# Setup of a decoder-trunk kernel: loads reordered over two queues, squares moved between the transposes, semaphores cleared by range

## The reference, cut to what matters

```python
mod = silu(c) @ w_mod[l] + b_mod[l]           # shift, scale, gate, 2 x 3 x 1024 columns, 9 vectors c
h = rms_norm(x, norm_mix[l]) * (1 + scale) + shift
x = x + gate * mixer(h)                       # layer 0: h @ ab_w_in first
```

## Time and profile before

| | us |
|---|---|
| runs (3) | 2413.52, 2416.56, 2420.88; median 2416.56 |
| the profiled execution | 2417.96 |
| its span, first to last instruction | 2416.3 |
| PE busy in the span | 2071.7 (86%) |
| DVE, ACT, POOL busy | 1360.7, 787.1, 272.1 |
| mean granted clock of PE | 0.913 |
| moved by DMA | 322.60 MB |

### The profile page before, as it was taken

The page is one execution under the profiler, slowest core; times in us unless marked ns, Lnnn a source line. Parts: engine busy times, 40 slices in busy tenths (PEclk is TensorE's granted clock), DMA queues, the critical chain, the costliest instruction groups (busy, mean ns, idle before and its releaser), DMA issues. The chain is left out here.

```text
span 2416.3 us, 48234 instructions
## 1 busy us (share of the span) xinstructions
PE 2071.7 (86%) x18117; PEld 1865.8 (77%) x18117; DVE 1360.7 (56%) x2556; ACT 787.1 (33%) x1407; POOL 272.1 (11%) x436
## 2 busy tenths in 40 slices
PE   4987797688999897997879996989987776999898
PEld 2873574386999896895569886988974475999898
DVE  3435431257888643446365657777743357888732
ACT  2211331114555301212246654544431214545300
POOL 0101333200000000000022212212223200000000
PEclk8996898798999998998789997999988898999999
DMA  8416789735333221224420004333449612333231
GB/s 345 131 45 254 246 294 365 283 111 159 97 98 106 96 87 40 62 83 181 174 91 1 2 1 145 112 105 113 118 140 339 237 62 70 105 100 93 90 96 62
DMA packets 237726, 322.60 MB, mean 134 GB/s; under 512 B 18235, under 2 KB 194440, under 8 KB 230063
## 3 DMA queue, kind: packets, MB, share of 16 engines
q1 hardware_dynamic: 215767, 240.34, 30.6%
q0 software_dynamic: 21728, 79.19, 9.5%
HBM read 311.56 MB, written 16.42 MB: 136 GB/s over the span
## 5 line engine op out<-in xcount | busy, mean ns | idle before, releaser
L2557 PE MATMUL ps<-CHi,W1H 128*128 128x256 f32 x768 | 221.7, 289 | 38.0 <-DVE CLo L2660 38.0
L2558 PE MATMUL ps<-CLo,W1H 128*128 128x256 f32 x768 | 219.7, 286 | 0.0
L2559 PE MATMUL ps<-CHi,W1L 128*128 128x256 f32 x768 | 219.5, 286 | 0.0
L897 PE MATMUL ps<-XHup,WLup 128*128 128x272 f32 x640 | 185.1, 289 | 0.0
L897 PE MATMUL ps<-XHup,WHup 128*128 128x272 f32 x640 | 183.8, 287 | 1.3 <-DVE G L1046 1.3
L897 PE MATMUL ps<-XLup,WHup 128*128 128x272 f32 x640 | 184.5, 288 | 0.0
L2557 PEld LDWEIGHTS ps<-CHi,W1H 128*128 128x128 f32 x768 | 150.0, 195 | 40.0 <-DVE CLo L2660 29.6
L443 PE MATMUL ps<-XHdn,WHdn 128*128 128x272 f32 x704 | 148.2, 292 | 14.7 <-DMA TOK<-in_cache_fox_v 6.5
L2078 DVE TENSOR_REDUCE NM<-ps 128x1 f32<-128x128 f32 (+1 forms) x224 | 89.6, 403 | 116.4 <-PE ps L1957 80.4
L2558 PEld LDWEIGHTS ps<-CLo,W1H 128*128 128x128 f32 x768 | 150.1, 195 | 0.0
L2559 PEld LDWEIGHTS ps<-CHi,W1L 128*128 128x128 f32 x768 | 149.9, 195 | 0.0
(11 more groups left out here) (562 smaller groups left out, 5339.6 us busy)
## 6 DMA issues: line engine op xcount, KB each, us to landing
H<-in_w_up SPq DMA_DIRECT2D x72, 512.0 KB, 4.9
Wearly<-in_w_mod SPq DMA_DIRECT2D x24, 1024.0 KB, 11.2
RAWdn<-in_w_down SPq DMA_DIRECT2D x14, 1408.0 KB, 6.3
RAWin<-in_nsa_w_in SPq DMA_DIRECT2D x20, 512.0 KB, 3.7
RINGf<-in_cache_fox_k SPq DMA_DIRECT2D x34, 256.0 KB, 5.6
Wmod<-in_w_mod SPq DMA_DIRECT2D x8, 1024.0 KB, 17.0
Wlate<-in_w_mod SPq DMA_DIRECT2D x8, 1024.0 KB, 8.3
G<-in_w_up SPq DMA_DIRECT2D x16, 512.0 KB, 5.4
```

Of the source, the lines that this page charges most:

```text
L897: last = self.nc.tensor.matmul(self.ps[:, bank + b, 0:HALF], wt[:, w, k, :], x[:, k, :], start=start and k == 0 and n == 0, stop=k == 3 an ...
L2557: nc.tensor.matmul(out, WH[:, sig, k, w], hi, start=(k == 0 and m == 0), stop=False, skip_group_check=True)
L2558: nc.tensor.matmul(out, WH[:, sig, k, w], lo, start=False, stop=False, skip_group_check=True)
L2559: last = nc.tensor.matmul(out, WL[:, sig, k, w], hi, start=False, stop=(k == KU - 1), skip_group_check=True)
```

## The change

Stages no longer clear their semaphores when they end. They are put on a list, and `flush`, called at the next stage's entry and at the end of the program, clears all of them in one block, with one `sem_clear` for each contiguous range of numbers.

In `setup`, SP issues the identity, the tokens, the ones, and the pieces of w_mod first; the first weight block comes as two halves (both in `self.first`), and the rest of the constants behind piece 1 of `Wearly`, under a semaphore of their own that the side job of the first projection waits for. The small vectors and the page table are issued by ACT. PE waits for identity, ones and tokens only, and for the vectors at k = 6. ACT makes every square into its own slice of H as soon as its group is there, and DVE adds them between the copies; scaling and page ids run in `root_dve`, while ACT computes the root. The bites before the first product are two instead of four, and `head_norm` takes 2 to 12 and loads 8 to 18.

```diff
@@ stage, clear
         nc = self.nc
+        self.flush()
         self.stages += 1
         number = self.stages
...
-            if made:
-                self.clear(made)
+        self.ended.append((semaphores, made))
+
+    def flush(self):
+
+        made = [s for _, m in self.ended for s in m]
+        if made:
+            self.clear(made)
+        while self.ended:
+            self.ended.pop()[0].close()
...
+                numbers = sorted(s.num for s in semaphores)
                 if drain:
-                    pool.dma_reset(range(min(s.num for s in semaphores), max(s.num for s in semaphores) + 1))
-                for s in semaphores:
-                    pool.sem_clear(s)
+                    pool.dma_reset(range(numbers[0], numbers[-1] + 1))
+                for a in numbers:
+                    if a - 1 not in numbers:
+                        pool.sem_clear(range(a, next(n + 1 for n in numbers if n >= a and n + 1 not in numbers)))
@@ setup, SP
-                    sp.dma_start(self.pages[:, :], i["page_table"].rearrange("(o b) n -> o (b n)", o=1)).then_inc(vec_in, 16)
-                    sp.dma_start(CN[:, :], i["const"][:, 0:CONST]).then_inc(c_in, 16)
...
+                    sp.dma_start(CN[:, 0:P], i["const"][:, 0:P]).then_inc(c_in, 16)
+                    sp.dma_start(XR[:, 0:4, :], i["x_prompt"][0].rearrange("(i p) d -> p i d", p=P)).then_inc(x_in, 16)
+                    sp.dma_start(XR[0:NS, 4, :], i["x_sample"].rearrange("b t d -> (b t) d")).then_inc(x_in, 16)
+                    sp.dma_start(CN[:, ones:ones + P], i["const"][:, ones:ones + P]).then_inc(c_in, 16)
                     for n in range(KD):
                         self.mod_load(sp, work, n)
-                    sp.dma_start(self.first_in[0], i["ab_w_in"][0:4 * P, 0:256].rearrange("(k p) n -> p k n", p=P)).then_inc(self.first_in[1], 16)
-                    for n in range(6):
+                    first_weights(sp, 0)
+                    for n in range(2):
+                        self.mod_load(sp, self.early, n)
+                    first_weights(sp, 1)
+                    sp.dma_start(CN[:, P:ones], i["const"][:, P:ones]).then_inc(self.const_in, 16)
+                    sp.dma_start(CN[:, ones + P:pmod - 1], i["const"][:, ones + P:pmod - 1]).then_inc(self.const_in, 16)
+                    for n in range(2, 6):
                         self.mod_load(sp, self.early, n)
@@ setup, ACT (12 DMAs are issued ahead of this: vectors, page table, pmod)
                     act.wait_ge(vec_in, 16 * n_vec)
                     nc.scalar.activation(R2[0:72, :], R2[0:72, :], ACT.Silu).then_inc(silu, 1)
                     for k in range(KD):
-                        act.wait_ge(xev, KD + 1)
-                        self.square(act, sums, k)
+                        act.wait_ge(xev, k + 2)
+                        nc.scalar.activation(self.H[:, k, :], X[:, k, :], ACT.Square).then_inc(sums["sq"], 1)
@@ setup, PE
-                    pe.wait_ge(c_in, 16)
-                    pe.wait_ge(vec_in, 16 * n_vec)
-                    nc.tensor.transpose(ps[:, 0, 0:P], R1[:, :], self.ident)
+                    pe.wait_ge(c_in, 32)
+                    pe.wait_ge(x_in, 32)
...
+                        if k == 6:
+                            pe.wait_ge(vec_in, 16 * n_vec)
+                            pe.wait_ge(silu, 1)
+                            nc.tensor.transpose(ps[:, 0, 0:P], R1[:, :], self.ident)
+                            nc.tensor.transpose(ps[:, 0, P:P + 82], R2[:, :], self.ident[0:82, 0:82]).then_inc(tr, 1)
@@ setup, DVE
+                    def square_sum(k):
+                        dve.wait_ge(sums["sq"], k + 1)
+                        link(nc.vector.tensor_tensor(self.H[:, self.SUM if k == KD - 1 else 0, :], self.H[:, 0, :], self.H[:, k, :], ALU.add))
...
                     for k in range(KD):
-                        dve.wait_ge(tr, k + 2)
+                        if k == 6:
+                            vectors_out()
+                        dve.wait_ge(tr, k + 2 + (k >= 6))
                         nc.vector.tensor_copy(X[:, k, 0:TP], ps[:, 2 + k % 6, :]).then_inc(xev, 1)
...
+                        if k >= 2:
+                            square_sum(k - 1)
+                    square_sum(KD - 1)
+                    dve.sem_inc(sums["added"], 1)
+                    self.root_dve(dve, link, root, small)
                     self.mod_add(dve, work, 0)
@@ fox_layer
-                self.linear("in", self.i["ab_w_in"], KD, 8, out=PT, norm=(0, 0), meal=(self.early, 0, 4, 4), first=self.first_in, root=self.root,
-                            more=lambda sp: [self.mod_load(sp, self.early, n) for n in range(6, 10)], beside=Forget(self, PT, NC, EP))
+                self.linear("in", self.i["ab_w_in"], KD, 8, out=PT, norm=(0, 0), meal=(self.early, 0, 2, 2), loaded=self.first_in, root=self.root,
+                            more=lambda sp: [self.mod_load(sp, self.early, n) for n in range(6, 8)], beside=Forget(self, PT, NC, EP))
...
-                               lambda sp: [self.mod_load(sp, self.early, n) for n in range(10, 19)], (self.early, 4, 13))
+                               lambda sp: [self.mod_load(sp, self.early, n) for n in range(8, 19)], (self.early, 2, 13))
```

More of the change, by code:

```diff
@@ L92, in __init__ @@
         self.stages = 0
+        self.ended = []
     @contextmanager
@@ L98, in stage @@
         nc = self.nc
+        self.flush()
         self.stages += 1
         number = self.stages
+        semaphores, made = ExitStack(), []
         with ExitStack() as held:
-            made = []
             def sb(name, shape, dt=F32):
@@ L107, in sem @@
             def sem(name):
-                made.append(held.enter_context(nc.semaphore(f"{name}_{number}")))
+                made.append(semaphores.enter_context(nc.semaphore(f"{name}_{number}")))
                 return made[-1]
             yield sb, sem
-            if made:
-                self.clear(made)
+        self.ended.append((semaphores, made))
[5 more added lines that the diff above has]
+            self.ended.pop()[0].close()
     def clear(self, semaphores, drain=True):
@@ L173, in setup, with first_weights @@
             work = self.mod_work("mod", sem, *meal_tile(sb("Wmod", [P, 512 + 8 * 2048])), [(0, 0)], [(4, 6)])
-            n_vec = 15
+            n_vec = 11
+            ones = 5 * P + 2 * NT + 4 * RUN
+            pmod = ones + P + PT_TILES * NCMP_P + 1 + NSEL + NS
+            def first_weights(sp, part):
+                sp.dma_start(self.first[:, part, :, :], i["ab_w_in"][part * 4 * P:(part + 1) * 4 * P, 0:256]
+                             .rearrange("(k p) n -> p k n", p=P)).then_inc(self.first_in[part], 16)
             with nc.Block() as block:
@@ L183, in _ @@
[L183 to L187, removed]
@@ L232, in _ @@
                         self.mod_bite(pe, work, n)
-                    pe.wait_ge(sums["added"], KD - 1)
+                    pe.wait_ge(sums["added"], 1)
                     self.root_pe(pe, root)
@@ L241, in _, with vectors_out @@
                     link = Chain(dve, dc)
+                    def square_sum(k):
+                        dve.wait_ge(sums["sq"], k + 1)
+                        link(nc.vector.tensor_tensor(self.H[:, self.SUM if k == KD - 1 else 0, :], self.H[:, 0, :], self.H[:, k, :], ALU.add))
+                    def vectors_out():
+                        dve.wait_ge(tr, 8)
+                        nc.vector.tensor_copy(VT[:, :], ps[:, 0, 0:P])
+                        nc.vector.memset(self.CV[:, :, :], 0.0)
+                        link(nc.vector.tensor_copy(CT[:, :], ps[:, 0, P:P + 82]))
+                        link(nc.vector.tensor_copy(self.CV[:, :, 0:9], CT[:, 0:72].rearrange("p (v k) -> p k v", k=KD)))
+                        dve.sem_inc(vectors, 1)
@@ new lines, in small @@
+                    def small():
+                        for c in (76, 78):
+                            nc.vector.tensor_scalar(CT[:, c:c + 1], CT[:, c:c + 1], SCALE, None, ALU.mult)
+                        dve.wait_ge(pg_in, 16)
+                        dve.wait_ge(pmod_in, 16)
+                        link(nc.vector.tensor_copy(PF[:, 0, :], PG[:, :]))
+                        link(nc.vector.tensor_scalar(PF[:, 0, :], PF[:, 0, :], float(CPP), self.pmod, ALU.mult, ALU.add))
+                        link(nc.vector.tensor_scalar(PF[:, 1, :], PF[:, 0, :], 2.0, None, ALU.mult))
+                        link(nc.vector.tensor_scalar(PF[:, 2, :], PF[:, 1, :], 1.0, None, ALU.add))
+                        link(nc.vector.tensor_copy(self.ids[:, :, :], PF[:, :, :]))
@@ L246, in _ @@
[L246 to L253, removed]
@@ L444, in product, with linear @@
         return mm
-    def linear(self, name, w, K, blocks, x=None, out=None, residual=None, norm=None, first=None, meal=None, more=None, beside=None, squares=False, root=None, into=None):
```

(14 more changed lines are left out.)

52 lines of the change are left out of this document (26 added, 26 removed).

## The result

The changed kernel takes 2379.63 us (median of 4 runs, 2377.38 to 2382.88) against 2416.62 beside it: ratio 0.9847, 95% interval 0.9827 to 0.9866, some 37 us less. Forecast were 2376 and 2361 to 2394. The profiled execution took 2380.61.

The account below looks back on a forecast made before the run. PE's products, busy 86% of the span, were taken as the bound, so only PE's idle time could go: setup -14.1, clears and blocks -32.3, head_norm +5.0, in sum -41.4 us, to 2376 us, range 2361 to 2394.

Parts of the forecast that it names:

- Clears by range: Clearing blocks: 440 single clears become some 25 range clears, -28.7 us; together with fewer blocks -32.3 us.
- rival 3: Clearing blocks: a range costs for each semaphore in it, 2393 to 2429 us, slower than before from 0.094 us each; chance 0.07.
- Rival 4: Clearing blocks: blocks or clears stay as many because numbers are scattered; half of the single clears left, 2391 us; chance 0.06.
- The eight blocks: Blocks directly behind another clearing block go, 29 become 21, at 0.45 us each: -3.6 us.
- Setup's start: Setup: tokens issued at about 1.3 us, so PE starts at 9.5 instead of 17.31, bounds 8 and 11.
- From the start to the norm's sum: Setup: 16.3 us of DVE work plus 1 for late squares, so the norm's sum starts at 26.8, not 39.75.
- Behind the sum: End of setup: root, bites and SP's issue (done at 31 to 35.3) end it at 35.5 instead of 49.56, -14.1 us.
- First projection: Stage behind setup: two bites fewer save nothing, weights arrive as before relative to the stage; zero, at worst +1 us.
- Head_norm: Head_norm: two more pieces land one after the other ahead of the products of line 1321, +5.0 us (+3 to +5.5).
- a rival of its own: Behind the clearing gaps: eight of twelve gaps lose their slow-clock stretch, -14 us, 2362; chance 0.07.
- Rival 1: Setup: the vectors on ACT's queue come late beside the full stream, 2383 us, or 2411 if behind all of it; chance 0.08.

Follow-up runs that it names:

- vectors_sp: The changed kernel with the twelve small loads issued by SP, behind the identity and ahead of the tokens, none by ACT: 2384.87 us, ratio 0.9869.
- short_issue: The changed kernel with sample tokens ahead of the prompt's, the ones under their own semaphore, pieces 4 and 5 loaded in the first projection: 2376.90 us, ratio 0.9852.
- squares_late: The changed kernel with squares and sums behind all copies, ACT and DVE taking turns again: 2384.39 us, ratio 0.9874.
- meal4: The changed kernel with the old split of bites, four before the first product and head_norm with 4 to 12: 2388.57 us, ratio 0.9881.
- clears_only: The kernel before with only the new stage ends (one flush per stage entry, one clear per contiguous range): 2391.24 us, ratio 0.9895.
- late_pieces: short_issue with pieces 2 to 7 of Wearly issued behind the weights of block 2 in the first projection: 2376.24 us, ratio 0.9827.

## Why the prediction was right

**Clears by range: right, over-estimated by 5.0 us.** 32.3 were forecast and 27.3 came. Two sizes were off. There are 54 ranges, not 25: eleven blocks have one, the other ten 2 to 8 (one in layer 1's attention has 8 and lasts 1.2 us). Probably nested stages reuse numbers that others have given back; the numbers themselves were not looked at. And a range does cost by its length: 0.286 us for the one of the 47-semaphore stage against 0.044 for the shortest, (0.286 - 0.044) / 46 = 0.005 us for each semaphore if the shortest holds one, 2.3 us for all 440; setup's 28 in one range took 0.181, on the same line. This is rival 3's mechanism at about an eighteenth of the price at which it would have turned the sign. Rival 4 is out: neither the blocks nor half of the single clears stayed. The eight blocks gave 3.7, forecast 3.6.

**Setup's start: too early by 3 us.** 9.5 was forecast and 12.47 came, beyond the bound of 11. The step took the tokens' 8.2 us from issue to landing over from the kernel before, but they took 9.7 to 10.3 (why is open, as said at vectors_sp), and PE also waits for the ones, issued fourth. The ones and the sample's place cost 1.6 us, by short_issue (10.89).

**From the start to the norm's sum: 15.1 instead of 17.3.** The silu was at 13.39, as forecast, but since PE was late it delayed nothing; and a copy and a sum together took 1.46 us (the first three sums start at 16.92, 18.38 and 19.84), not 1.75. That 27.54 came so near to 26.8 is luck: PE's start was 3 us late, and the way from there 2.2 us short. What the squares' move is worth is shown by squares_late: 5.5 us at the norm's sum and 6.0 in setup, against some 6 by the seven idle times of 0.87.

**Behind the sum: right in the path, a little early.** SP's own issue did end last, at 36.55, forecast 31 to 35.3; compute was done at 35.18. The end of setup was forecast at 35.5, and the reset came at 36.9. The upper end of 35.3 does not even follow from its own figures (13.4 MB at 0.42 MB a us from 2.3 us on are 34.2). The megabytes were right (13.3 by 37 us); the rate was not 420 GB/s from the start, but 236 in the first 10 us and 390 in the next 10. PE did have the full clock behind the sum (five bites in 4.50 us instead of 5.99, the norm's sum in 1.19 instead of 2.18).

**First projection: the number right, the reason wrong.** "Two bites fewer ahead of it save nothing" may hold for the kernel before, where PE waited for DVE anyway; no run has it with two bites. In the kernel after, where the stage starts 14 us earlier and the queue is still full, they save 8 us, as meal4 shows. I had worked out that block 1's weights come as late relative to the stage as before; they came nearly 5 us later (60.9 - 37.5 = 23.4, before 70.5 - 51.9 = 18.6), and PE still had no wait for them. The step had 21.7 MB landed at 54, by 420 GB/s; the trace has 22.6 MB by 61, a mean of 370. That the stage came out near zero is luck. The step also compared the old and the new order, but not the new setup with the old meal.

**Head_norm: the arrival right, the price hidden by the clock.** The last bite started 26.6 us into the stage instead of 21.9, +4.7 for the forecast +5.0. But the stage grew by 1.6 only. Behind the last bite it took 11.1 us instead of 13.4, because PE had its full clock for part of it: 0.72 on average, where the same stretch before was all at the half level. clears_only, which has the old meal, shows what the stage costs when the clock is mostly up, 32.0 us instead of 37.2 with the same work. The windows of that last part, before and in clears_only:

```profile
196.30:209.50 13.20, 11.65 (x40) 7.38 (x36) 6.11 (x9) 0.00 (x0) 0.00 (x0) 0.50 0.90 376
```

```profile
188.70:198.90 10.20, 8.40 (x40) 5.44 (x36) 6.20 (x9) 0.00 (x0) 0.00 (x0) 0.82 1.02 423
```

The same holds for the new meal. squares_late has it, with its late bites at the full clock too; the last bite of clears_only and that of squares_late:

```profile
187.72 1.06 PE L303 MATMUL ps<-Wearly,CV 128*32 128x512 f32 x8 [1.44 <-DMA Wearly<-in_w_mod]
```

```profile
185.63 1.06 PE L334 MATMUL ps<-Wearly,CV 128*32 128x512 f32 x8 [1.43 <-DMA Wearly<-in_w_mod]
```

These start 20.7 and 25.6 us into their stages, which take 32.0 and 37.9. So with a like clock up to that bite the two bites cost 4.9 us of arrival and 5.9 of the stage, as forecast; the 1.6 of the changed kernel is a price of 5 less what a luckier clock gave. It made up for two thirds of what the clears fell short by (3.4 of 5.0), and that is luck.

I had given the clock to a rival of its own, with -14 us over the whole kernel. Its mean did rise, 0.913 to 0.916, and in clears_only to 0.918; but behind 19 of the 20 gaps of PE around clearing blocks that another product follows, the clock granted over the next 7 us was still only 0.50 to 0.80, in the changed kernel as before, and the stages without an edit did not become faster (+2.1 in sum). The Trainium skill (TensorE: Matmul & The Clock Gate, "What's actually happening") says that the clock follows PE's recent activity and that the moment at which it changes depends on where in the gate's own, free-running rhythm the products begin. Two head_norm stages fit the second half, though they do not show it: with the same gap of 4.21 us ahead of it, the stage had a mean clock of 0.71 in the changed kernel and 0.86 in clears_only, each from some 7 us into the stage to its first product behind the bites.

**The vectors** were not starved: the silu started at 13.39. Rival 1 is out for this order of loads. The Trainium skill (DMA: Bandwidth & Descriptors, "Queues, rings and completion order") has the engines take turns between queues; by the silu's start the trace agrees.

## What to carry to other kernels

Work that all engines wait for costs its full length however small its pieces are: 29 blocks with 440 clears of 0.04 us took 41.4 us, and 27.3 of it could go. When a prefix becomes shorter while a queue of loads is full, ask of everything behind it how many bytes stand ahead of its load, and move out of the queue's head what is not needed yet; the gain is else given back one stage later (meal4, short_issue). Bites that wait for loads belong between other work of the same engine, not ahead of it: in head_norm's stage that gave 8.5 us, though the whole time does not show it yet.

## What the runs showed of the hardware that was not expected

- A range clear takes longer with its length: 0.044 us for the shortest, 0.181 for 28 semaphores, 0.286 for 47.
- With the stream still queued, a DMA instruction of a few bytes can hold its issuing engine as long as large ones: `FB`, a vector, took 11.68 us to issue on SP in the changed kernel (37.97 to 49.65), 6.51 in short_issue and 2.71 in late_pieces, where fewer pieces are queued ahead, against 0.48 before, where the stream had landed. The load just ahead of it, 32 KB, took 0.38 in the changed kernel.

```profile
37.97 11.68 SPq L1118 DMA_DIRECT2D FB<-in_ab_b_fgate  x1
```

- Stages without an edit differed by 8.6 us in sum between two profiled executions of the changed kernel (stages 7 to 21: 1915.3 and 1906.7), more than most single steps of this change are worth.
